# Rounded weight tiles and constants 192 bytes further on, two clears ahead of a scan, one gate tile rounded a step sooner

## What is computed

```python
def first_block(x, ...):
    proj = x @ w_in + b_in                      # 1024 x 5632, split in nine
    y_a = hgrn2_mixer(hg_q, hg_f, hg_i, hg_g, ...) @ w_proj_a
    y_b = moba_mixer(mb_q, mb_k, mb_v, rel_bias) @ w_proj_b
    mixed = (sigmoid(gate_a) * y_a + sigmoid(gate_b) * y_b) @ w_out
    x = layer_norm(DN_ALPHA * x + mixed, ln1_g, ln1_b)
    ffn = hier_moe(x, w_group, b_group, w_expert, b_expert, w_gate_up, w_down)
    return layer_norm(DN_ALPHA * x + ffn, ln2_g, ln2_b)

def second_block(x, meta, ...):
    h = concatenate([meta, x])                  # 272 rows
    for i, mixer in enumerate((pool_mixer, sb_mixer)):
        h = h + mixer(rmsnorm(h, norm_mix[i]))
        a = rmsnorm(h, norm_ffn[i])
        h = h + (silu(a @ w_gate[i]) * (a @ w_up[i])) @ w_down[i]
    return rmsnorm(h, final_norm)[:, 16:]
```

## Time and profile before

| | us |
|---|---|
| median of 3 runs | 1198.43 (1197.92 to 1202.88) |
| the profiled execution | 1200.12 |
| its span, first to last instruction | 1198.8 |
| TensorE busy | 1064.6 |
| VectorE busy | 583.2 |
| ScalarE busy | 479.2 |
| GpSimd busy | 86.2 |

### The profile page before, as it was taken

One profiled execution on the slowest core, in us unless ns is written; L12 is line 12 of the kernel. 1 busy time (PEld: TensorE's weight loads), 2 busy tenths in 40 slices (PEclk: granted clock), 3 DMA queues, 4 the chain that ended last, 5 costly groups with the idle time before them and its releaser, 6 DMA issues.

```text
span 1198.8 us, 21347 instructions
## 1 busy us (share of the span) xinstructions
PE 1064.6 (89%) x9288; PEld 873.9 (73%) x9288; DVE 583.2 (49%) x846; ACT 479.2 (40%) x652; POOL 86.2 (7%) x83
## 2 busy tenths in 40 slices
PE   8999999997567776766677999999999999999998
PEld 8899998653333333333333899999999999999986
DVE  5775777642212121212113676664454557666633
ACT  6654863221111111111124643443457765544433
POOL 1640002000000000000000400000210005000000
PEclk9999999998887778778878999999999999999999
DMA  9843579999999999999999676454634236665430
GB/s 367 308 153 114 186 277 421 390 420 427 427 428 427 428 426 428 426 427 420 423 428 391 190 241 203 157 185 159 197 112 132 89 109 203 199 211 177 175 106 36
DMA packets 104220, 330.28 MB, mean 276 GB/s; under 512 B 4339, under 2 KB 76332, under 8 KB 86334
## 3 DMA queue, kind: packets, MB, share of 16 engines
q1 hardware_dynamic: 102064, 322.77, 70.0%
q10 hardware_dynamic: 1470, 4.02, 0.9%
q0 software_dynamic: 592, 2.10, 0.6%
HBM read 327.82 MB, written 1.06 MB: 274 GB/s over the span
## 4 chain that ended last, share of the span: by engine, by line
PE 62%; DMA 31%; DVE 3%; ACT 3%; issue 1%; SPq 0%; ACTq 0%; DVEq 0%
DMA wide<-in_w_gate_up_dram 15%; DMA wide<-in_w_down_dram 14%; PE PS L489 13%; PE PS L490 12%; PE PS L491 12%; PE PS L1225 5%; PE PS L854 3%; PE PS L504 2%; PE PS L505 2%; PE PS L506 2%; PE PS L848 2%; DMA raw<-in_w_down_dram 1%; PE PS L592 1%; DMA raw<-in_w_in_dram 1%; DVE lo L1988 1%
## 5 line engine op out<-in xcount | busy, mean ns | idle before, releaser
L1988 DVE TENSOR_TENSOR lo<-raw,hi 128x2048 fp32r<-128x2048 f32 (+1 forms) x111 | 253.4, 2289 | 141.8 <-ACT hi L1473 123.3
L1473 ACT CAST hi<-raw 128x2048 fp32r<-128x2048 f32 (+1 forms) x109 | 203.7, 1874 | 109.8 <-PE PS L491 75.4
L489 PE MATMUL PS<-AH,hi 128*128 128x256 f32 (+1 forms) x816 | 233.7, 286 | 1.7 <-DVE AL L2481 1.0
L490 PE MATMUL PS<-AL,hi 128*128 128x256 f32 (+1 forms) x816 | 231.2, 283 | 0.0
L491 PE MATMUL PS<-AH,lo 128*128 128x256 f32 (+1 forms) x816 | 231.1, 283 | 0.0
L854 PE MATMUL PS<-wide,XS 128*32 128x256 f32 x1568 | 132.8, 495 | 86.3 <-DMA wide<-in_w_gate_up_dram 82.7
L854 PEld LDWEIGHTS PS<-wide,XS 128*32 128x32 f32 x1568 | 59.0, 134 | 147.1 <-DMA wide<-in_w_gate_up_dram 100.2
L489 PEld LDWEIGHTS PS<-AH,hi 128*128 128x128 f32 x816 | 154.8, 190 | 3.2 <-issue 1.0
L490 PEld LDWEIGHTS PS<-AL,hi 128*128 128x128 f32 x816 | 153.7, 188 | 0.4
L491 PEld LDWEIGHTS PS<-AH,lo 128*128 128x128 f32 x816 | 153.7, 188 | 0.0
L2400 DVE TENSOR_TENSOR T<-T,PS 64x256 f32<-64x256 f32 x32 | 13.5, 423 | 205.5 <-ACT T L1677 205.4
(11 more groups left out here) (443 smaller groups left out, 1865.8 us busy)
## 6 DMA issues: line engine op xcount, KB each, us to landing
wide<-in_w_gate_up_dram SPq DMA_DIRECT2D x49, 2048.0 KB, 46.0
wide<-in_w_down_dram SPq DMA_DIRECT2D x25, 2048.0 KB, 45.0
raw<-in_ffn_w_gate_dram SPq DMA_DIRECT2D x22, 1024.0 KB, 5.4
raw<-in_ffn_w_up_dram SPq DMA_DIRECT2D x22, 1024.0 KB, 5.7
raw<-in_w_in_dram SPq DMA_DIRECT2D x21, 1024.0 KB, 8.4
raw<-in_ffn_w_down_dram SPq DMA_DIRECT2D x19, 1024.0 KB, 5.0
spare<-in_w_gate_up_dram SPq DMA_DIRECT2D x14, 1024.0 KB, 12.9
raw<-in_sb_w_qkv_dram SPq DMA_DIRECT2D x12, 1024.0 KB, 5.1
```

The source lines that it names most:

```text
L489: pe.matmul(o, w(h, c), xh(k), start=start and c == c0, stop=False)
L490: pe.matmul(o, w(h, c), xl(k), start=False, stop=False)
L1473: act.copy(K.view(K.hi[i % HN], 0, [[1, n]]), K.view(K.rbuf[i], 0, [[1, n]])).then_inc(S.hi, 1)
L1988: r = e.tensor_tensor(K.view(K.lo[i % HN], 0, [[1, n]]), K.view(K.rbuf[i], 0, [[1, n]]), K.view(K.hi[i % HN], 0, [[1, n]]).bitcast(F32), A ...
```

## The change

Three edits. (1) A new constant `HB = 48 KB + 192` takes the place of 48 KB for hi, lo, the halves (alone and in the wide tiles) and, 48 KB further on, cm, pc, small and flag with the small tiles on the masks. Raw tiles and all from A0 on stay. (2) The clears of AA0 and AA1 stand ahead of the wait for the logarithm and the scan instead of behind it. (3) In feed-forward 1 the gate tile of step 3 is rounded by ScalarE in step 1, behind the up tile of step 2 and ahead of silu; VectorE takes its rest in step 1 behind the product, ahead of FL. Both leave it out in step 2.

```diff
+    HB = 48 * KB + 192
...
-    K.hi = [sb(f"hi{i}", 2048, 48 * KB + 8 * KB * i, F32R) for i in range(HN)]
-    K.lo = [sb(f"lo{i}", 2048, 72 * KB + 8 * KB * i, F32R) for i in range(HN)]
-    K.cm = sb("cm", CMW, 96 * KB)
+    K.hi = [sb(f"hi{i}", 2048, HB + 8 * KB * i, F32R) for i in range(HN)]
+    K.lo = [sb(f"lo{i}", 2048, HB + (24 + 8 * i) * KB, F32R) for i in range(HN)]
+    K.cm = sb("cm", CMW, HB + 48 * KB)
...
-    masks = 96 * KB + 4 * CM["masks"][0]
+    masks = HB + 48 * KB + 4 * CM["masks"][0]
...
-    halves = [sb(f"half{i}", 2048, 48 * KB + 8 * KB * off) for i, off in enumerate((0, 3, 1, 4, 2, 5))]
+    halves = [sb(f"half{i}", 2048, HB + 8 * KB * off) for i, off in enumerate((0, 3, 1, 4, 2, 5))]
...
@@ act_ffn
-        if f != 1:
+        if f != 1 and not (i and f == 2):
             act_ahead(act, K, S, K.at["fg", (i, f)])
         act_ahead(act, K, S, K.at["fu", (i, f)])
-        if f == 0:
-            act_ahead(act, K, S, K.at["fg", (i, 1)])
+        if f == 0 or (i and f == 1):
+            act_ahead(act, K, S, K.at["fg", (i, f + 1)])
@@ dve_mixers
     gates_f(1)
+    dve.memset(K.AA0[:, :], 0.0)
+    zeroed = own(dve.memset(K.AA1[:, :], 0.0))
     dve.wait_ge(S.act_step, STEP["f_log"])
     dve.wait_ge(S.scn, 16)
     dve.tensor_tensor_scan(K.BT[:, :], K.SCN[:, :], K.BT[:, :], 0.0, ALU.mult, ALU.add).then_inc(S.dve_step, 1)
-    dve.memset(K.AA0[:, :], 0.0)
-    zeroed = own(dve.memset(K.AA1[:, :], 0.0))
@@ dve_ffn
-        if f != 1:
+        if f != 1 and not (i and f == 2):
             dve_ahead(dve, K, S, n, K.NU)
...
         dve.tensor_tensor(xa, xa, xb, ALU.mult).then_inc(S.f_prod, 1)
+        if i and f == 1:
+            dve_ahead(dve, K, S, K.at["fg", (i, 2)], K.NU)
```

More of the change, by code:

```diff
@@ L231, in memory @@
     K.raw = [sb(f"raw{i}", 2048, 8 * KB * i) for i in range(RN)]
-    K.hi = [sb(f"hi{i}", 2048, 48 * KB + 8 * KB * i, F32R) for i in range(HN)]
-    K.lo = [sb(f"lo{i}", 2048, 72 * KB + 8 * KB * i, F32R) for i in range(HN)]
-    K.cm = sb("cm", CMW, 96 * KB)
-    K.pc = sb("pc", PCW, 96 * KB + 7936)
-    K.small = sb("small", 128, 96 * KB + 7936 + 512)
-    K.flag = sb("flag", 8, 96 * KB + 7936 + 1024, U32)
+    K.hi = [sb(f"hi{i}", 2048, HB + 8 * KB * i, F32R) for i in range(HN)]
+    K.lo = [sb(f"lo{i}", 2048, HB + (24 + 8 * i) * KB, F32R) for i in range(HN)]
+    K.cm = sb("cm", CMW, HB + 48 * KB)
+    K.pc = sb("pc", PCW, HB + 48 * KB + 7936)
+    K.small = sb("small", 128, HB + 48 * KB + 7936 + 512)
+    K.flag = sb("flag", 8, HB + 48 * KB + 7936 + 1024, U32)
     def con(name, off=0, w=None, p0=0, rows=128):
@@ L399, in memory @@
             ("half0", "half2"), ("half4", "half1"), ("half3", "half5"), ("early6", "early4")]
-    at_base = (A0 + 32 * KB, 0, A0 + 80 * KB, 16 * KB, A0 + 64 * KB, 32 * KB, 48 * KB, 64 * KB, 80 * KB, A0 + 8 * KB)
+    at_base = (A0 + 32 * KB, 0, A0 + 80 * KB, 16 * KB, A0 + 64 * KB, 32 * KB, HB, HB + 16 * KB, HB + 32 * KB, A0 + 8 * KB)
     kept = (1, 3, 5, 6, 7, 8)
```

## The result

The kernel before ran in 1198.69 us in the comparison (median of 5 runs), the changed one in 1209.91 us (median of 5, 1208.30 to 1210.29). The ratio is 1.0078, interval 1.0062 to 1.0094: **0.8% slower**, outside the predicted range of 1184 to 1205 us and on the other side of the forecast. The profiled execution has a span of 1208.6 us against 1198.8.

What follows compares the result with a forecast made beforehand. TensorE was taken to bound the kernel, except from 268 to 640 us, where DMA did. Terms -0.8 - 1.0 - 3.5 - 1.0 = -6.3 us, from the 1198.4 us median, gave 1192.1 us; range 1184 to 1205 us.

Steps and rivals of the forecast that it cites:

- (3), the place: Tile addresses: Q leaves distance 0, V and the down stream leave 64, other spacings stay; -1.0 us, bounds -10.6 and +9.2.
- rival E: All 256-column streams held at Q's 120 ns by distance 0: +7.5 us net, 1205.9 us; chance 0.20.
- step 2: Last gated layer's gate tile: wait at 1041 us goes, -1.0 us; fast 113.3 ns spacing then lasts, -3.5 us.
- (1), the clears: Around the scan near 30 us: clears fit VectorE's idle time, the next rest starts earlier, TensorE waits less; -0.8 us.
- Rival B: Tile addresses are neutral for matmul spacing; only the clears and gate tile count: -5.3 us, 1193.1 us; chance 0.15.
- Rival D: New distance removes most collisions: -5.3 and half to all of -10.6 us, 1182.5 to 1187.8 us; chance 0.20.

Runs made afterwards that it cites:

- the two moves alone: Changed kernel with rounded weights, rests and constants back at 48 KB, keeping clears and gate tile moved: 1195.59 us, ratio 0.9967; second series 1196.87 us, 0.9982.
- isolated rows: Kernel computation left out, only rows of 48 fp32r matmuls with streams and weights at varied byte offsets; 256 columns: 120.0 ns at distance 0, 113.3 at 192.

## Why the prediction was wrong

**(3), the place, is the step that failed.** The bounds were -10.6 and +9.2 us and I took -1.0, because "the effects have both signs, and I find no row that fixes one". There was such a row: Q in the earlier trace rows, the one stream that had the new distance, at 120 ns. The value should have been taken by it, and that is rival E. I held against it that Q also has another chunk length; but of all that differs between Q and its neighbours K and V, the distance was the one thing the change was about to give to everyone. It also was the only row *at the new value*. FH's and AH's rows, which made me think of gains, were at old distances. What failed in the prediction's own words is "the fast and slow spacings of the rest stay as they are": every fast and every slow one became 120.0 ns. Measured, the term is +12.2 us against the kernel before. The sum, though, adds it to step 2, which had already given the last layer back its fast spacing; from there, the two moves alone, the same table gives +14.7 us (6.6 instead of 3.6 for the last layer, 4.2 instead of 3.9 for the mixers), and the span grew by 13.3.

**E's price was too small too**, 1205.9 us against 1209.9. Its parts for 256 columns were right: +9.2 put, +9.5 measured (3.9, 2.0 and 3.6). What it left out were the 272-column streams (+2.4), the 512-column ones (+0.6 and -0.3), and V less Q (0.0): I had priced them only in the gain's direction, though the earlier trace rows showed them to depend on place as well. A bound has to be drawn for every group of rows on both sides.

**(1), the clears:** the mechanism was right (rest at 29.12, predicted 28.95; TensorE late next). Its size was 0.48 us in the changed kernel (L505 at 32.25 for 32.73) instead of 0.76, since TensorE itself comes later by then. In the two moves alone, where it doesn't, L505 starts at 31.88 us: 0.85. And the wait itself, 0.77 us in the first profile of the kernel before, is 1.16 and 1.22 us in the other two at full clock and 1.64 with the gate tile alone. The bound of -0.8 was drawn from one profile.

**(2), the gate tile:** the wait is gone, as reckoned, with the gate tile alone and with the two moves alone (-1.0; in the changed kernel the new place would have taken it away too). The 3.5 us for the lasting fast spacing were sized rightly as long as the distance stays (113.3 ns in the two moves alone), but the reason was wrong: that a stall spoils the spacing came from a single wait in a single profile. The same wait in the kernel with the clears alone spoils nothing, and the settling matmul that was to bring the fast spacing didn't bring it at one of its two places in four of nine profiles. And 1.2 us of it go back in the down projection, a term that the sum didn't have. Steps 1 and 2 together: -5.3 put; in the two series of the two moves the ratios give -4.0 and -2.2 us, the medians -4.5 (1195.59 against 1200.08) and -2.9 (1196.87 against 1199.79).

**Rival B** had beside it the rule of the Trainium skill (TensorE: Matmul & The Clock Gate, "Step-by-step: what each phase is for"), which says that the two SBUF read ports are independent and that loading the next weights takes nothing from the running matmul. The isolated rows disagree: with nothing else running, moving only the stream against the weights takes a matmul of 256 columns from 113.3 to 120.0 ns. The measurement decides: two reads whose relative place sets the pace aren't independent. Which of the two is held up, and by what, isn't shown.

**Rival D**'s bound of -10.6 us had -6.1 in it for 272 columns, from FH's shortest records. There was nothing to win there: by the isolated rows distance 192, where AH already lay, is the fastest of the four (123.4 ns). A record isn't a spacing.

**The range** left out what happened: E's lower part was cut off at 1205 although its own sum was 1205.9, and the bounds of step 3 with both moves worth nothing gave 1207.6 (1198.4 + 9.2). With what the groups that E left out measured (+2.4, +0.6 and -0.3) its sum would have been 1208.6.

## What to carry to other kernels

When a change moves tiles, write down for every pair of tiles that one instruction reads together the distance modulo 256 bytes before and after, and look in the trace for any pair that already has the new distance: its spacing is the forecast to start from, even if it differs in other ways. Do it for every reader of a tile: FL won 1.2 us in one stage and lost 0.6 in another. In these runs fp32r streams of 256 and 272 columns were fastest 192 bytes further on than the weights, streams of 512 columns at 0 or 64; for other shapes measure it in isolated rows, which takes one run. Where a distance has two spacings (64 and 192 here), count with both. Don't infer from one wait in one profile what a wait does to the pace behind it.

## What the runs showed that I had not expected

- A 256-column fp32r matmul follows its neighbour after 113.3, 117.8, 118.6 or 120.0 ns at full clock, that is 256 columns and 16 to 32 cycles at 2.4 GHz. Moving one of two tiles by a few dozen bytes is enough to change it, with no other engine running.
- At distances 64 and 192 there are two spacings, 113.3 and 117.8 ns. In the isolated rows at 192 all five blocks behind a 384-column matmul were fast and one of five behind a wait was slow (weights at 0, 64, 128, 192 and stream distance 192 or 448); at 64 the one fast block of four was behind a wait. In the kernels the last 16 units of gate and up tiles keep the one that they start with.
- The best distance for 256 columns (192) is among the worst for 512 (233.3 ns against 227 at 0).
- A slower TensorE hides its own waits: with the new place the 1.5 us of waits that two edits were to take away had gone without them, but for 0.3 us. And a wait isn't a constant: with the same code up to there, the one at 32 us was 0.77 to 1.64 us long.
